# The last stage of an encoder layer joined to the program of its experts, and tokens' ranks dealt over the places of a block

## The reference

```
x = x + g1 * (concat[att, rec] @ w_out)
h = rms_norm(x, norm2_g) * (1 + sc2) + sh2
x = x + g2 * hmoe(h)          # top-1 of 4 groups, then top-2 of its 8 experts
y = rms_norm(x, final_g)
...
hid = silu(xb @ w1[e]) * (xb @ w3[e])      # 1024 -> 512, 32 experts
out[tok] += (hid @ w2[e]) * wt             # 512 -> 1024
```

## Time and profile before

| what | value |
|---|---|
| median of 3 runs | 1489.77 us (1484.55 to 1494.36) |
| the profiled execution, device time | 1494.64 us |
| its span, from the first to the last instruction | 1492.4 us |
| PE busy | 1182.9 us, 79% |
| DVE, ACT, POOL busy | 28%, 23%, 19% |
| moved by DMA | 314.73 MB, mean 211 GB/s |
| mean granted TensorE clock | 0.917 |

### The profile page before, as it was taken

The page is one execution under the profiler, slowest core; times in us unless marked ns, Lnnn a source line. Parts: engine busy times, 40 slices in busy tenths (PEclk is TensorE's granted clock), DMA queues, the critical chain, the costliest instruction groups (busy, mean ns, idle before and its releaser), DMA issues. The chain is left out here.

```text
span 1492.4 us, 29866 instructions
## 1 busy us (share of the span) xinstructions
PE 1182.9 (79%) x13181; PEld 736.2 (49%) x13181; DVE 420.8 (28%) x709; ACT 341.1 (23%) x722; POOL 287.0 (19%) x231
## 2 busy tenths in 40 slices
PE   5999999999957878878739983998877878788830
PEld 3555555554536767767634552554444434444410
DVE  2100234335643444445452324000000000000017
ACT  3200033443323435444411120110010010100005
POOL 0100012212334333334280000111111111111003
PEclk8999999999986999999959985999999999988975
DMA  9793303123323112120056119999999999999934
GB/s 320 284 316 142 114 29 107 50 78 113 118 79 67 46 25 46 24 46 4 4 211 249 40 73 377 386 387 403 395 398 411 411 409 394 400 397 400 384 134 166
DMA packets 77609, 314.73 MB, mean 211 GB/s; under 512 B 9674, under 2 KB 24354, under 8 KB 60734
## 3 DMA queue, kind: packets, MB, share of 16 engines
q1 hardware_dynamic: 71446, 298.94, 53.6%
q0 software_dynamic: 5120, 12.59, 2.5%
q10 hardware_dynamic: 936, 1.61, 0.3%
HBM read 291.56 MB, written 25.74 MB: 213 GB/s over the span
## 5 line engine op out<-in xcount | busy, mean ns | idle before, releaser
L2257 PE MATMUL bank<-arena 128*64 128x256 f32 x2048 | 260.7, 414 | 71.1 <-DMA arena<-in_exp_w 60.1
L1480 PE MATMUL bank<-arena 64*64 64x64 f32 (+3 forms) x7344 | 217.0, 222 | 75.2 <-DVE arena L1382 17.3
L894 PE MATMUL bank<-arena 128*128 128x512 f32 (+1 forms) x736 | 258.3, 500 | 4.1 <-DVE arena L485 2.0
L2257 PEld LDWEIGHTS bank<-arena 128*64 128x64 f32 x2048 | 160.2, 149 | 180.8 <-DMA arena<-in_exp_w 70.9
L1480 PEld LDWEIGHTS bank<-arena 64*64 64x64 f32 (+2 forms) x7344 | 191.3, 127 | 103.2 <-issue 56.4
L894 PEld LDWEIGHTS bank<-arena 128*128 128x128 f32 x736 | 135.0, 191 | 100.2 <-issue 85.0
L2275 PE MATMUL bank<-arena 128*64 128x512 f32 x512 | 116.9, 598 | 16.8 <-ACT arena L2200 16.8
L2148 POOL DMA_INDIRECT arena<-h_scratch,arena x32 | 30.7, 960 | 417.7 <-PE bank L2244 285.3
L2223 DVE TENSOR_TENSOR arena<-bank,arena 128x256 f32<-128x256 f32 x32 | 13.6, 425 | 315.1 <-PE bank L2257 315.1
L2014 PE MATMUL bank<-arena 128*128 128x512 f32 x192 | 86.7, 607 | 1.9 <-PEq L2396 1.9
L2275 PEld LDWEIGHTS bank<-arena 128*64 128x64 f32 x512 | 34.1, 136 | 77.5 <-issue 54.7
(11 more groups left out here) (253 smaller groups left out, 1258.0 us busy)
## 6 DMA issues: line engine op xcount, KB each, us to landing
arena<-in_exp_w SPq DMA_DIRECT2D x96, 2048.0 KB, 45.2
arena<-in_ada_w SPq DMA_DIRECT2D x12, 2048.0 KB
arena<-in_w_in SPq DMA_DIRECT2D x11, 1024.0 KB, 8.5
direction_scratch<-arena SPq DMA_DIRECT2D x6, 1536.0 KB, 5.5
arena<-direction_scratch SPq DMA_DIRECT2D x24, 384.0 KB, 5.4
arena<-pick_out SPq DMA_DIRECT2D x6, 1024.0 KB, 11.6
arena<-in_x_sample SPq DMA_DIRECT2D x8, 512.0 KB, 5.9
arena<-mod_scratch SPq DMA_DIRECT2D x8, 512.0 KB, 9.9
```

The source lines that it names most:

```text
L894: return nc.tensor.matmul(bank[i % 3][:, 0:GR[p] * GW], w[:, k, :], hT[:, k, PART[p]], start=(k == 0), stop=(k == KD - 1))
L1480: return nc.tensor.matmul(out, lhsT, r, start=start, stop=True, skip_group_check=True)
L2257: ins = nc.tensor.matmul(bank[b + 2 * c.s][BLK * n:BLK * n + BLK, 0:HALF], xT[c.s][:, j, :], slot[c.w][:, j, n * HALF:(n + 1) * HALF], sta ...
```

## The change

**The last stage becomes part of the third program.** The drain, the two barriers and the clearing of semaphores between them are gone. GpSimd, after its last put has landed and after the jump over its overflow code, raises `picks_out`, and SP waits for that before it loads `ya`. SP issues the load of `f_row` earlier, after PE's product with w2 for the last expert but two. The places of `f_row` and its neighbours in the on-chip memory move, since the experts' buffers are still in use.

**GpSimd's products and ACT's `unit` are gone.** DVE does both products of every tile in one instruction (`final`), as it did for the last tile alone.

**The number of overflow blocks is read earlier.** `overflow_count` waits for `list_out` and loads the register; `overflow` then takes the register. ACT and DVE call it ahead of their loop over the experts, GpSimd ahead of its last three puts, SP ahead of its wait for the last expert, PE still behind its loop. ACT's wait for the landing of the last put at the end of its loop is gone.

**Ranks are dealt over the places.** `rank_row` was 0, 1, 2, ..., 63; it is now 0, 16, 32, 48, 1, 17, 33, 49, ..., so that rank r stands at place 4 (r mod 16) + r div 16.

```
-    row = [..., np.zeros(1), np.arange(BLK), np.arange(NBLK) * BLK, ...]
+    row = [..., np.zeros(1), np.arange(BLK).reshape(4, BLK // 4).T.ravel(), np.arange(NBLK) * BLK, ...]
...
+        def overflow_count(eng):
+            eng.wait_ge(sem("list_out"), 16)
+            return eng.value_load(over_dram[0:1, 1:2], min_val=0, max_val=MAX_OVER)
...
 sp_phase6
-            sp.wait_ge(sem("g2_in"), 32)
-            sp.wait_ge(sem("list_out"), 16)
             sp.wait_ge(sem("over_slots_out"), 32)
+            count = overflow_count(sp)
+            sp.wait_ge(sem("y_mm6"), CREDIT + NE - 2)
+            sp.dma_start(f_row, A["final_row"].partition_broadcast(P)).then_inc(sem("final_in"), 16)
             sp.wait_ge(sem("y_mm6"), CREDIT + NE)
-            overflow(sp, over, with_expert=True)
+            overflow(sp, over, count, with_expert=True)
...
 pool_phase6
+            count = overflow_count(pool)
             for e in range(NE - 3, NE):
                 freed(e - 1)
                 put(e)
...
-            pool.wait_ge(sem("list_out"), 16)
-            overflow(pool, gather)
+            overflow(pool, gather, count)
+            pool.sem_inc(sem("picks_out"), 1)
...
 act_phase6
+            count = overflow_count(act)
             rows(Main(0, 0, 0, 0, 0, 0))
             turns(act, body, ahead=1, pairs=True)
-            act.wait_ge(sem("yb_free"), CREDIT + NE)
...
 dve_phase6
+            count = overflow_count(dve)
             turns(dve, body)
...
 sp_phase7
+            sp.wait_ge(sem("picks_out"), 1)
             for t in range(NT):
                 sp.dma_start(ya[t], picks[t]).then_inc(sem(f"rows_in{t}"), 16)
-                if t == 0:
-                    sp.dma_start(f_row, A["final_row"].partition_broadcast(P)).then_inc(sem("final_in"), 16)
...
-        def pool_phase7(pool):
-            pool.wait_ge(sem("final_in"), 16)
-            for t in range(NT - 1):
-                pool.wait_ge(sem("unit_ready"), t + 1)
-                nc.gpsimd.tensor_tensor(yo[t], yo[t], f_row, ALU.mult).then_inc(sem("final_ready"), 1)
...
 dve_phase7
-            def root(t):
+            def final(t):
                 dve.wait_ge(sem("act_own7"), 2 * t + 2)
-                nc.vector.reciprocal(stat7[:, t, 2:3], stat7[:, t, 1:2]).then_inc(sem("root_inv"), 1)
+                own.link(nc.vector.reciprocal(stat7[:, t, 2:3], stat7[:, t, 1:2]))
+                dve.wait_ge(sem("joined"), t + 1)
+                nc.vector.scalar_tensor_tensor(yo[t], x2[:, t, :], stat7[:, t, 2:3], f_row, ALU.mult, ALU.mult).then_inc(sem("final_ready"), 1)
...
                          (sp_phase4, pool_phase4, act_phase4, dve_phase4, pe_phase4),
-                         (sp_router_experts, pool_router_experts, act_router_experts, dve_router_experts, pe_router_experts),
-                         (sp_phase7, pool_phase7, act_phase7, dve_phase7, None))[:upto]:
+                         (sp_router_experts, pool_router_experts, act_router_experts, dve_router_experts, pe_router_experts))[:upto]:
```

More of the change, by code:

```diff
@@ L118, in constants @@
     e = np.arange(NE, dtype=np.float32)
-    row = [e, e * BLK, 8.0 - np.arange(8), np.zeros(1), np.arange(BLK), np.arange(NBLK) * BLK, np.zeros(2 * NT), np.zeros(NE), np.zeros(1)]
+    row = [e, e * BLK, 8.0 - np.arange(8), np.zeros(1), np.arange(BLK).reshape(4, BLK // 4).T.ravel(), np.arange(NBLK) * BLK, np.zeros(2 * NT), np.zeros(NE), np.zeros(1)]
     route = np.tile(np.concatenate(row).astype(np.float32), (P, 1))
@@ L2095, in turns, with overflow @@
                 body(block(whole, u), *([None if last else block(whole, u + 1)] if pairs else []))
-        def overflow(eng, body, with_expert=False):
-            count = eng.value_load(over_dram[0:1, 1:2], min_val=0, max_val=MAX_OVER)
+        def overflow_count(eng):
+            eng.wait_ge(sem("list_out"), 16)
+            return eng.value_load(over_dram[0:1, 1:2], min_val=0, max_val=MAX_OVER)
+        def overflow(eng, body, count, with_expert=False):
             with eng.If(count > 0):
@@ L2209, in over @@
                 act.wait_ge(sem("over_done"), c.n + 2)
-            overflow(act, over)
+            overflow(act, over, count)
         def dve_phase6(dve):
@@ L2227, in body @@
                 nc.vector.tensor_copy(yb[c.s], bank[6 + c.s]).then_inc(c.sem("y_ready6"), 1)
+            count = overflow_count(dve)
             turns(dve, body)
-            overflow(dve, body)
+            overflow(dve, body, count)
         def pe_phase6(pe):
@@ L2284, in pe_phase6 @@
             turns(pe, body, ahead=1, pairs=True)
-            overflow(pe, over)
-        top[0] = base6
+            overflow(pe, over, overflow_count(pe))
+        top[0] = ARENA - 2 * WEXP
+        ya = [take(2 * D).rearrange("p (k d) -> p k d", k=2) for _ in range(NT)]
+        yo = [take(D) for _ in range(NT)]
+        top[0] = P + 2
         f_row = take(D)
@@ L2291, in build @@
         stat7 = take(NT * 4).rearrange("p (t m) -> p t m", t=NT)
[L2292 to L2295, removed]
         y_out_v = [O[1][0, t * P:(t + 1) * P, :] for t in range(NT_S)] + [O[0][0, t * P:(t + 1) * P, :] for t in range(NT_P)]
@@ L2299, in sp_phase7 @@
             picks = y_dram.rearrange("(k t p h) n -> t p k (h n)", k=2, t=NT, p=P)
+            sp.wait_ge(sem("picks_out"), 1)
             for t in range(NT):
                 sp.dma_start(ya[t], picks[t]).then_inc(sem(f"rows_in{t}"), 16)
-                if t == 0:
-                    sp.dma_start(f_row, A["final_row"].partition_broadcast(P)).then_inc(sem("final_in"), 16)
             for t in range(NT):
[L2305 to L2308, removed]
+                sp.wait_ge(sem("final_ready"), t + 1)
                 sp.dma_start(y_out_v[t], yo[t]).then_inc(sem("final_out"), 16)
             sp.wait_ge(sem("final_out"), 16 * NT)
-        def pool_phase7(pool):
-            pool.wait_ge(sem("final_in"), 16)
-            for t in range(NT - 1):
-                pool.wait_ge(sem("unit_ready"), t + 1)
-                nc.gpsimd.tensor_tensor(yo[t], yo[t], f_row, ALU.mult).then_inc(sem("final_ready"), 1)
         def act_phase7(act):
@@ L2324, in first_row @@
                 nc.scalar.mul(ya[t][:, 0], ya[t][:, 0], wts[:, t, 0:1]).then_inc(sem("first_scaled"), 1)
-            def unit(t):
-                act.wait_ge(sem("root_inv"), t + 1)
-                nc.scalar.mul(yo[t], x2[:, t, :], stat7[:, t, 2:3]).then_inc(sem("unit_ready"), 1)
+            act.wait_ge(sem("list_ready"), 1)
             first_row(0)
@@ L2340, in act_phase7 @@
                     first_row(t + 2)
-                if t:
-                    unit(t - 1)
         def dve_phase7(dve):
@@ L2346, in dve_phase7 @@
             dve.wait_ge(sem("final_in"), 16)
+            dve.wait_ge(sem("g2_in"), 32)
             def join(t):
@@ L2362, in dve_phase7 @@
                 if t:
[L2363 to L2366, removed]
+                    final(t - 1)
+            final(NT - 1)
         def sp_router_experts(sp):
@@ L2371, in sp_router_experts @@
             sp_phase6(sp)
+            sp_phase7(sp)
         def pool_router_experts(pool):
@@ L2379, in act_router_experts @@
             act_phase6(act)
+            act_phase7(act)
         def dve_router_experts(dve):
@@ L2383, in dve_router_experts @@
             dve_phase6(dve)
+            dve_phase7(dve)
         def pe_router_experts(pe):
```

## The result

The changed kernel takes 1480.82 us, median of 18 runs (1476.19 to 1490.47), the kernel before 1493.19 (18 runs, 1484.17 to 1499.08). The ratio is 0.9931 with a 95% interval of 0.9916 to 0.9947: 0.69% or 10.3 us faster, where 6.9 us were forecast. (The two medians lie 12.4 us apart; the text goes by the recorded ratio, from which the quotient of the medians differs by up to 0.0014 here and in the experiments.) The profiled execution of the changed kernel took 1480.52 us, its span 1478.8.

A forecast was written before the change was run, and what follows sets the result against it. The DMA engines' weight stream, 201 MB at about 400 GB/s, was taken as the bound, followed by a serial tail. Terms -13.0 + 9.6 - 3.5 = -6.9 us off the median of 1489.77 gave 1483 us, range 1475 to 1491.

The forecast's parts named there:

- the three mechanisms: The prediction's summed terms: shorter tail -13.0 us, early read of the count +9.6, dealing of ranks -3.5.
- The tail: From last put to the end: barrier, start of joins, DVE's work and stores save 13.0 us, between 11 and 14.
- The barrier's part: Between last put and SP's first load of picked rows: load at 1436.3 instead of 1443.68, saving 7.4 us.
- what follows the load: After SP's first load of picked rows: DVE begins 5.4 + 1.2 us later, works 32.1, end 4.4 after.
- DVE's work: Last stage without GpSimd's products: joins 23.0 us, four finals 6.1, ACT's square and root 1.5, last final 1.5: 32.1.
- The early read: ACT's count read ahead of its first copy waits for the list: copy at 933.3 instead of 923.71, 9.6 us later.
- a list that lands early: Rival at the expert stage's start: list there at 920.5, ACT loses only 0.7 us; sum -15.8, 1474 us; chance 0.10.
- one that comes last in its queue: Forecast's choice at the expert stage's start: list lands behind a 2 MB weight transfer at 932.2, costing 9.6 us.
- The dealing: Ragged end of the weight stream: puts levelled, gathers not, half of 10.2 us less some loss: -3.5 us.
- two landings, of 8.0 and 9.6 us: Gathers with 28 and 64 picks; their unequal landings were read as gathers already dealt more finely than by fours.
- Crowding, the slower rival: Dealt ranks share DMA engines (place modulo 16), stream ends 10.4 us later; sum +7.0, 1497 us; chance 0.10.
- The signs named beforehand: Profile after: first copy near 933 us, DMA gap some 9, shorter end fall, joins 1.28, put to end some 46.

The follow-up runs named there:

- e6: Changed kernel with ACT's count read behind its expert loop and ranks in order, so only the tail's change: 1481.23 us, ratio to before 0.9913.
- e9: Changed kernel with the overflow list's transfer issued ahead of the 2 MB weight load just before it, read still early: 1479.53 us, ratio to before 0.9910.
- e3: Kernel before with only the ranks dealt as in the changed kernel: 1485.77 us, ratio to before 0.9961.
- e4: Changed kernel with ranks dealt by pairs of places instead of by fours: 1477.35 us, ratio to before 0.9901.
- e5: Changed kernel with ACT's count read behind its expert loop and ranks dealt by pairs: 1467.19 us, ratio to before 0.9835.
- e1: Changed kernel with ACT reading the overflow count behind its loop over the experts again: 1472.33 us, ratio to before 0.9855.
- e2: Changed kernel with ranks 0, 1, 2, ... in order over the places again: 1484.68 us, ratio to before 0.9942.

## Why the prediction held, and where its sizes were off

The direction and the three mechanisms were right, and the time lies in the range. The forecast of 6.9 us is short of the 10.3 measured (7.9 to 12.5 by the interval). That the absolute time came closer, 1483 against 1480.8 us, is in part luck: it was taken off a median of three runs, 1489.77 us, and off the 1493.19 of the 18 runs it would have been 1486.3. Point by point:

**The tail**, forecast -13.0, measured -14.9 (e6: -14.6). The barrier's part was right: between last put and SP's first load lie 3.0 us instead of 10.4, 7.4 were forecast. Too small was what follows the load: 48.7 us before, 41.3 now, a gain of 7.4 where the terms made it 5.6. DVE begins 6.3 us behind the load (6.6 forecast), its chain takes 1443.76 to 1474.73 = 31.0 us (32.1 forecast, since I took a join with its gap as 3.84 us and a final as 1.52, and they take 3.71 and 1.39), and the end follows 4.1 us later (4.4). It is the term "DVE's work" that was mis-sized most, by 1.1 us.

**The early read**, forecast +9.6. At the first copy it is nearly that: 15.4 us behind the list's issue, against 6.2 before, 9.2 us, and the refill of the slots stands 22.4 us behind it, against 12.3. The choice between a list that lands early and one that comes last in its queue was the main one of the prediction; 14.2 us to the read, and 8.6 in e9 with 2 MB less ahead of it, show that the order of the queue holds it. The Trainium skill (DMA: Bandwidth & Descriptors, section Queues, rings and completion order) says that each engine consumes a queue's descriptors in ring order; the trace agrees, with 5.6 us for the 2 MB. In the DMA engines' idle time it is as forecast too: 10.4 to 10.8 us are lost in the first 40 us with the early read, 0.4 to 1.2 without, and the share in the middle is 1.01 in all. By the last put, however, the early read costs less: the streams with it are longer by 7.7 us with ranks in order (523.65 against 515.75 to 516.31), 9.3 dealt by fours (520.05 and 520.62 against 512.15 and 509.90) and 5.5 by pairs (514.12 against 508.62). What is made up is not idle time: from the list to the last put the packets, without those of `f_row`, took the engines 504.3 to 505.1 us in the six kernels in which ACT reads late and 501.8 to 504.5 in the four with the early read, 1.7 us less on average. Why the same transfers took less stays open.

**The dealing**, forecast -3.5, too small. By the stream it is 3.3 us with the early read and 4.9 with the late one, 5.8 us by the time of e3, and by the loss in the last window of the two profiles, without `f_row`, 10.13 - 5.97 = 4.16 us. The reason given, that puts become level and gathers do not, is borne out as far as the deals tell: fours win 4 to 5 of the some 10 us of the ragged end, pairs about 8 (e4, e5). The Trainium skill (DMA: Bandwidth & Descriptors, section The descriptor swizzle) speaks of groups of four consecutive partitions for a transfer over 128; the puts are such, and the half that fours win agrees. The gathers, over 64 partitions, don't go by groups of four here: by the estimate under e4 the deal by pairs would then have left 5.3 us, and it left 1.6 to 2.4. Gathers and puts were not dealt apart from each other, since both go by the place; so that the other half is the gathers' is worked out from three deals and the routing, not shown by itself. The forecast read it off two landings, of 8.0 and 9.6 us, which was thin evidence. Crowding, the slower rival, did not come: e3 is faster than before.

**The signs named beforehand**: the count read ahead of the first copy, a gap in the DMA share (10.3 us against 9 to 10), a shorter fall of it at the end, joins of 1.22 to 1.28 us, a first load right behind the landing of the last put, 44.3 us from the last put to the end where 46 were named. All are there. The sum of the profile is -14.86 + 4.30 = -10.6 us: of the 3.7 us that the forecast lacks, 1.9 are the tail's and 1.8 the stream's, where +9.6 - 3.5 = +6.1 had been forecast. In the stream 0.4 us more were lost at its start than forecast and 0.7 less at its end, and the engines were busy 1.6 us less with the same transfers, for which the forecast had no term.

## What to carry to other kernels

Count a change's parts apart: here one line that moved a read of 0.8 us gave back 5 to 9 of the some 18 us that the rest won (e1), because the word that it reads was queued behind megabytes of weights. Place the reader of such a word where it loses nothing by waiting (e1). Issuing the small transfer ahead of bulk loads helps too: ahead of one load of 2 MB the stream was 3.6 us shorter (e9); ahead of all of them was not tried. Where a stream of bulk transfers ends raggedly, look at which places of the small indirect transfers are filled: an order of the rows alone, with no byte less, shortened the stream by 7 to 10 us here (e4 against e2, e5 against e6).

## What the runs showed that was not expected

- The read of one word from HBM into a register took 0.64 us in the tail of before and 0.81 us in the changed kernel, both with the DMA engines idle, but 2.5 us in e9, where they were busy with the weights behind the list (share 0.96 over those 2.5 us), and 3.4 us for DVE in e1 (share 0.66). A busy share alone is not the cause: in the changed kernel GpSimd read the same word in 0.69 us while the share was 1.15 (a packet counts whole where it begins). The two lines are DVE's of e1 and GpSimd's of the changed kernel; what sets the long reads apart stays open.

```profile
L2099 DVEq TENSOR_LOAD <-overflow_list x1: 3419/3419/3419, 928.3 to 928.3; - x1
```

```profile
L2099 POOLq TENSOR_LOAD <-overflow_list x1: 692/692/692, 1387.1 to 1387.1; - x1
```

- The gather's rows can be levelled over the DMA engines by pairs of places: the DMA share in the 20 us window near the end of the stream is 0.94 to 0.98 with pairs dealt, 0.75 to 0.77 with fours, 0.49 to 0.56 in order.
- Up to the issue of the list, in code that is the same in all eleven kernels but for e9's one moved transfer and the numbers in `rank_row`, executions differ by up to 8.3 us (910.8 to 919.2 us): the two parts behind it had to be compared by themselves.
